# Attention values in the last mixer of a two-block network: V stationary, outputs transposed, another order of the queues

## The reference

```python
def masked_softmax(s, mask):
    s = jnp.where(mask, s.astype(jnp.float32), NEG)
    m = jnp.max(s, axis=-1, keepdims=True)
    p = jnp.where(mask, jnp.exp(s - m), 0.0)
    return p / jnp.maximum(jnp.sum(p, axis=-1, keepdims=True), 1e-30)

    proj = xn @ w_in[l]              # 1024 -> 5400: all inputs of both mixers
    y_a = hgrn2_mixer(a_q, a_f, a_i, a_g, lb_all[l], hgrn_norm_g[l])
    y_b = nsa_mixer(b_q, kc, vc, ks_, vs_, kw_, vw_, b_gate, positions, ...)
...
        # in nsa_mixer, for 8 heads of width 64 in 2 groups of 4
        o_c = p_c @ vc               # 15 compressed blocks
        o_s = p_s @ v_sel            # selected blocks
        o_w = p_w @ v_w              # window of 512
        return gb[..., 0:1] * o_c + gb[..., 1:2] * o_s + gb[..., 2:3] * o_w
...
    g_a, g_b = jnp.split(jax.nn.sigmoid(m_gate), 2, axis=-1)
    merged = g_a * (y_a @ w_br_a[l]) + g_b * (y_b @ w_br_b[l])
    h = h + merged @ w_out[l]
    hn = rmsnorm(h, norm2_g[l])
    h = h + jnp.square(jax.nn.relu(hn @ w_ff1[l])) @ w_ff2[l]
```

## Time and profile before

| | |
|---|---|
| median of 3 runs | 1398.23 us (1398.12 to 1399.13) |
| the profiled execution, its time | 1401.26 us |
| its span, first to last instruction | 1399.5 us |
| outside the span | 1.8 us |
| mean granted TensorE clock | 0.993 |
| TensorE busy | 1371.5 us, 98% |
| VectorE busy | 809.1 us, 58% |
| ScalarE busy | 680.6 us, 49% |

### The profile page before, as it was taken

One profiled execution on the slowest core, in us unless ns is written; L12 is line 12 of the kernel. 1 busy time (PEld: TensorE's weight loads), 2 busy tenths in 40 slices (PEclk: granted clock), 3 DMA queues, 4 the chain that ended last, 5 costly groups with the idle time before them and its releaser, 6 DMA issues.

```text
span 1399.5 us, 17400 instructions
## 1 busy us (share of the span) xinstructions
PE 1371.5 (98%) x6529; PEld 1125.6 (80%) x6529; DVE 809.1 (58%) x889; ACT 680.6 (49%) x877; POOL 37.5 (3%) x100
## 2 busy tenths in 40 slices
PE   8999999999999999999999999999999989999997
PEld 6888888888888888888877788888787778888886
DVE  5555566664555655444578754456676547664553
ACT  5444464454444644444467644445663555543442
POOL 2000000000000000000001100000000000000000
PEclk9999999999999999999999999999999989999999
DMA  8665656545656554555751365565553333565540
GB/s 288 212 195 185 212 179 210 178 139 184 195 191 225 180 180 150 182 187 196 240 172 55 112 208 182 187 196 200 198 181 121 107 138 121 184 237 180 180 165 30
DMA packets 160236, 247.09 MB, mean 177 GB/s; under 512 B 9086, under 2 KB 104504, under 8 KB 160184
## 3 DMA queue, kind: packets, MB, share of 16 engines
q1 hardware_dynamic: 160072, 246.33, 53.2%
q10 hardware_dynamic: 112, 0.05, 0.0%
HBM read 245.30 MB, written 1.05 MB: 176 GB/s over the span
## 4 chain that ended last, share of the span: by engine, by line
PE 95%; ACT 3%; DVE 1%; issue 0%; DMA 0%; POOL 0%; SPq 0%; POOLq 0%; ACTq 0%; DVEq 0%
PE GU L557 15%; PE GU L559 15%; PE GU L558 15%; PE DD L557 11%; PE DD L559 11%; PE DD L558 11%; PE GU L622 4%; PE TB L594 3%; PE TB L750 2%; PE GU L629 2%; ACT xh L1532 1%; PE DD L1185 0%; ACT whi L1520 0%; DMA raw<-in_w_ffn_up 0%; ACT sm L1921 0%
## 5 line engine op out<-in xcount | busy, mean ns | idle before, releaser
L2130 DVE TENSOR_TENSOR wlo<-raw,whi 128x2048 fp32r<-128x2048 f32 x224 | 509.3, 2282 | 273.4 <-ACT whi L1520 273.2
L1520 ACT ACTIVATE whi<-raw 128x2048 fp32r<-128x2048 f32 x223 | 424.2, 1908 | 176.8 <-PE DD L559 166.5
L557 PE MATMUL GU<-whi,xh 128*128 128x512 f32 (+1 forms) x944 | 373.1, 395 | 0.5 <-DVE hid L2247 0.5
L559 PE MATMUL GU<-whi,xl 128*128 128x512 f32 (+1 forms) x944 | 367.5, 389 | 0.0
L558 PE MATMUL GU<-wlo,xh 128*128 128x512 f32 (+1 forms) x944 | 366.3, 388 | 0.0
L559 PEld LDWEIGHTS GU<-whi,xl 128*128 128x128 f32 x944 | 177.5, 188 | 37.5
L557 PEld LDWEIGHTS GU<-whi,xh 128*128 128x128 f32 x944 | 177.7, 188 | 36.7 <-issue 2.1
L558 PEld LDWEIGHTS GU<-wlo,xh 128*128 128x128 f32 x944 | 177.9, 188 | 34.5
L557 PE MATMUL DD<-whi,hth 128*128 128x512 f32 x496 | 194.7, 393 | 0.0
L559 PE MATMUL DD<-whi,htl 128*128 128x512 f32 x496 | 193.2, 390 | 0.0
L558 PE MATMUL DD<-wlo,hth 128*128 128x512 f32 x496 | 193.1, 389 | 0.0
(11 more groups left out here) (300 smaller groups left out, 1082.6 us busy)
## 6 DMA issues: line engine op xcount, KB each, us to landing
raw<-in_w_ffn_down SPq DMA_DIRECT2D x88, 512.0 KB, 4.4
raw<-in_w_ffn_gate SPq DMA_DIRECT2D x86, 512.0 KB, 4.0
raw<-in_w_ffn_up SPq DMA_DIRECT2D x86, 512.0 KB, 5.0
raw<-in_w_ff SPq DMA_DIRECT2D x64, 512.0 KB, 4.4
raw<-in_w_in SPq DMA_DIRECT2D x40, 512.0 KB, 4.6
raw<-in_w_conv_in SPq DMA_DIRECT2D x24, 512.0 KB, 4.9
raw<-in_w_kv SPq DMA_DIRECT2D x16, 512.0 KB, 4.7
raw<-in_w_conv_out SPq DMA_DIRECT2D x8, 512.0 KB, 4.9
```

What stands on the lines that cost most here:

```text
L557: pe.matmul(dst, h, w_h, start=start, stop=False)
L559: return pe.matmul(dst, l, w_h, start=False, stop=stop)
L1520: nc.scalar.activation(whi[s][:, 0:size], raw[s][:, 0:size], ACT.Copy).then_inc(hi_done[s], 1)
L2130: nc.vector.tensor_tensor(wlo[s][:, 0:size], raw[s][:, 0:size], whi[s][:, 0:size].bitcast(F32), ALU.subtract).then_inc(lo_done[s], 1)
```

## The change

Five things are changed, all in the mixer stage.

1. `values(u)` makes V stationary (128 keys x 64 columns) and streams the transposed probabilities, 256 columns for the first 128 keys and 128 columns for the second. The two heads of a unit go into columns 0 to 63 and 64 to 127 of the array and so into the two halves of the PSUM partitions. There are four matmuls instead of six, and the result is the transposed output.
2. Since the rows are no longer on the partitions there, the gate over the sum is applied earlier: `normalise(u)` on VectorE multiplies the probabilities in `sm` with it, two instructions of 2 x 128 and 2 x 256 columns, and `probs_t(u, c)` waits for that (`norm_ready`) instead of for `exp_done`. `outputs(u)` becomes a copy of 128 x 256 into `yT` for units 0 to 3 and an addition for units 4 to 7; `add_outputs` is gone.
3. `block_values` is turned in the same way (four matmuls of 256 columns), the gate goes into the block probabilities, and `block_outputs(b)` is one addition of 128 x 512 for each half.
4. The attention's output is thus already transposed. The two `fill(yb, b)` with their eight transposes are gone, and `high_sums(b)` and `low_sums(b)` split it from SBUF, 128 x 512 each.
5. Group 10 of the projection accumulates in `DD` instead of `GU` (`win_bank`), which lets it go ahead of `block_values`. The orders on the three engines are written anew.

```diff
-        yb = hid[:, :, :]
+        yT = hid[:, :, :].rearrange("p t (a n) -> p (t a) n", n=S)
...
+        def win_bank(g):
+            return DD if g == 10 else GU
...
                 def probs_t(u, c):
-                    pe.wait_ge(exp_done, u + 1)
+                    pe.wait_ge(norm_ready, u + 1)
                     bank_transposes(c, [(q * P, sm[:, u % 2, c, q * P:(q + 1) * P]) for q in range(3)])
...
-                    for i in range(2):
-                        lo_ = 3 * P * i
-                        o0, o1 = (slice((2 * i + q) * 64, (2 * i + q) * 64 + 64) for q in range(2))
-                        pe.matmul(TB[:, b, o0], at[:, b, lo_:lo_ + P], vals[:, 0, :], start=True, stop=True)
-                        pe.matmul(TB[:, b, o1], at[:, b, lo_ + P:lo_ + 2 * P], vals[:, 0, :], start=True, stop=False)
-                        mm = pe.matmul(TB[:, b, o1], at[:, b, lo_ + 2 * P:lo_ + 3 * P], vals[:, 1, :], start=False, stop=True)
+                    for c in range(2):
+                        pe.matmul(TB[64 * c:64 * c + 64, b, 0:S], vals[:, 0, :], at[:, b, 3 * P * c:3 * P * c + S], start=True, stop=False)
+                    for c in range(2):
+                        mm = pe.matmul(TB[64 * c:64 * c + 64, b, P:S], vals[:, 1, :], at[:, b, 3 * P * c + S:3 * P * (c + 1)],
+                                       start=False, stop=True)
...
-                    for t in range(TT):
-                        mm = pe.matmul(GU[:, t, :], pcT[:, t * P:(t + 1) * P], vbd, start=True, stop=True)
+                    for j in range(4):
+                        mm = pe.matmul(GU[:, j // 2, S * (j % 2):S * (j % 2) + S], vbd[:, j * P:(j + 1) * P], pcT, start=True, stop=True)
...
                 compress(0, 0)
-                probs_t(3, 0)
                 compress(0, 1)
-                values(2)
                 pe.wait_ge(t_used[1], spot(base, "tk3"))
                 scores(4)
-                probs_t(3, 1)
+                values(2)
                 compress(1, 0)
                 compress(1, 1)
-                values(3)
+                probs_t(3, 0)
+                probs_t(3, 1)
                 hidden_sums(0)
                 scores(5)
                 pe.wait_ge(parts_ready, 2)
                 win(9, "a0")
                 hidden_sums(1)
-                scores(6)
+                values(3)
                 probs_t(4, 0)
                 win(9, "a1")
+                scores(6)
...
                 probs_t(6, 1)
+                win(10, "a0")
                 values(5)
                 probs_t(7, 0)
+                win(10, "a1")
                 block_probs_t()
+                probs_t(7, 1)
...
                 block_values()
-                probs_t(7, 1)
                 values(6)
                 values(7)
-                pe.wait_ge(oc_used, 1)
-                win(10, "a0")
                 pe.wait_ge(ya_ready, 1)
                 fill(ya, 0)
-                win(10, "a1")
                 fill(ya, 1)
                 win(10, "b0")
                 win(10, "b1")
-                pe.wait_ge(yb_ready, 1)
-                fill(yb, 0)
-                fill(yb, 1)
+                pe.wait_ge(yb_ready, 2)
...
                 for t in range(TT):
                     pe.wait_ge(gu_used[t], n.gu)
                 branch(0, 0)
...
+                def high_sums(b):
+                    act.wait_ge(yb_ready, b + 1)
+                    nc.scalar.activation(xh[:, 4 + 2 * b:6 + 2 * b, :], yT[:, 2 * b:2 * b + 2, :], ACT.Copy).then_inc(xh_done, 1)
...
+                def normalise(u):
                     dve.wait_ge(exp_done, u + 1)
                     chain(nc.vector.reciprocal(rdn8[:, u, :, :], den8[:, u, :, :]))
                     gv = gate_cols[:, :, 3 * 2 * j + br + 1:3 * (2 * j + 2):3].rearrange("p t i -> p i t")
                     chain(nc.vector.tensor_tensor(wgt8[:, u, :, :], rdn8[:, u, :, :], gv, ALU.mult))
+                    p4 = sm[:, b, :, :].rearrange("p c (k n) -> p c k n", n=P)
+                    for q, ks in ((0, slice(0, 1)), (1, slice(1, 3))):
+                        ins = nc.vector.tensor_tensor(p4[:, :, ks, :], p4[:, :, ks, :],
+                                                      wgt8[:, u, :, q:q + 1].unsqueeze(3).broadcast_to([P, 2, q + 1, P]), ALU.mult)
+                    ins.then_inc(norm_ready, 1)
+
+                def outputs(u):
...
+                    if br == 0:
+                        nc.vector.tensor_copy(yT[:, j, :], TB[:, b, 0:S]).then_inc(t_used[b], 1)
+                    else:
+                        dve.wait_ge(t_used[b], spot(base, f"V{j}"))
+                        nc.vector.tensor_tensor(yT[:, j, :], yT[:, j, :], TB[:, b, 0:S], ALU.add).then_inc(t_used[b], 1)
```

94 lines of the change are left out of this document (45 added, 49 removed).

## The result

The changed kernel takes 1393.35 us in the median of 8 runs (1390.72 to 1394.77), the kernel before 1398.43 us (8 runs). The ratio is 0.995, with a 95% interval from 0.9936 to 0.9963: faster, by 5.1 us in the medians. The forecast was 1392.1.

A forecast was written before the change was run, and what follows sets the result against it. TensorE, busy 98% of the span, was taken as the bound. Values -2.3, fills -0.2, waits 0, clock -2.8 and -0.8 for waits vanishing at low clock sum to -6.1 us: 1398.2 to 1392.1 us, range 1388.0 to 1396.8.

The forecast's parts named there:

- Values: Eight values units on TensorE: 10.1 us before, 1.02 us each after, 7.8 us in all, so -2.3 us.
- The rival of the loads: Values units: eight loads of V, 134 ns each, not hidden; 2.1 us a unit, +2.5 us in all, 1400.7; chance 4%.
- The rival of heads in turn: Values units: the two heads run one after the other, +3.1 for -2.3 us, 1397.5 in all; chance 8%.
- Fills: Ahead of branch(0, 0): 0.97 us of yb fills go, a 0.8 us wait for group 10's copy comes; -0.2 us.
- Waits: TensorE's waits in the mixer stage: sum 4.7 us as before, so 0 us; bounds -2 to +3.
- (a): At hidden_sums(0): TensorE waits 1.6 us for the copy of unit 3's transposes, behind a split waiting for its load.
- (b): At values(3): TensorE waits 1.6 us, its bank shared with hidden_sums(1), read behind the second split, exps(4) and a table load.
- Clock: Mixer stage: two low stretches of 3.44 us lose 3.4 us where 6.2 us were lost before; -2.8 us.
- Normalise: VectorE, between exps and transposes: some 1.0 us a unit, 8 us in all, free in amount; unit 4 closest.
- No low clock in the stage: Rival for the mixer stage: all 6.2 us of low-clock loss goes; -8.4 us in all, 1389.8; chance 14%.
- Waits take the gain: Rival: normalise or the splits end 1 to 1.5 us later at three places; +3 us, 1395.1; chance 12%.
- spreading clock: Rival: three thin places each bring a stretch like the 10.24 us one; +4.8 us in all, 1403; chance 6%.

The follow-up runs named there:

- e7: Changed kernel with both heads of a unit in the same column group, head by head; 1395.41 us, ratio 0.9976.
- e11: Kernel before without the two fills of yb, xh and xl split from hid as it lies; 1401.1 us, ratio 1.0007.
- e9: Changed kernel without normalise's two multiplications, transposes waiting for the exponentials alone; 1391.72 us, ratio 0.9936.
- e5: Changed kernel timed again without any edit, in a later group of runs; 1393.36 us, ratio 0.9957.
- e3: Changed kernel with twelve unread matmuls of 512 columns put ahead of hidden_sums(0), where TensorE waited; 1391.09 us, ratio 0.9927.
- e2: Changed kernel with the first two parts of group 10's projection moved back behind values(7); 1397.98 us, ratio 0.998.
- e1: Changed kernel's new arithmetic with the orders of the kernel before on all three engines; 1399.33 us, ratio 0.9984.
- e10: Changed kernel with normalise's multiplications done twice in each of the eight units; 1395.49 us, ratio 0.9961.

## Why the prediction was right, and where it was off

**The sign, the size and the range.** 1393.35 us for a forecast of 1392.1, within 1388.0 to 1396.8 and within the forecast's own range of times. Its condition of a unit between 0.85 and 1.15 us was not met, with 0.80. Two terms were off by more than a microsecond, and against the median they were off in opposite ways: values gave more than forecast, and the clock gave next to nothing there. That the sum came out within 1.3 us is in part luck.

**Values: -3.8 us, not -2.3.** This is the mis-sized term. Eight units are about 6.3 us (six at 0.80 or 0.81, units 6 and 7 together about 1.5) for 10.1. The mechanism held: 384 columns are 0.67 us, as one head alone in e7 shows with its 0.65 us a head, and the two heads run side by side. What failed was the price of the switch, 0.35 us a unit, taken from matmuls of 128 columns. Here it is 0.80 - 0.67 = 0.13 us. What this rest is made of, no run separates; that it was called a switch is the prediction's reading. In e7 it is 1.45 - 2 x 0.67 = 0.11 us, with one column group, so the residue doesn't come from the second group. The Trainium skill, TensorEngine Tiling (Array Packing), section Theoretical Speedup, with its 2x, would have made the term, as an estimate, -5.0 us; the measured -3.8 lies between it and the forecast. The two heads by themselves do come near it, 1.45 / 0.80 = 1.8.

**The rival of the loads** (8 x 134 ns not hidden) has fallen: a unit of 0.80 us has no room for 0.67 us of columns and 1.07 us of loads in turn. By the rule on row groups in the Trainium skill, TensorE: Matmul & The Clock Gate, Part 3, The mechanism, these loads would not overlap; this trace doesn't agree, with the same 0.80 us. The rival of heads in turn is what e7 is, and e7 is what it would have looked like.

**Fills: -0.2 us, right to the digit.** The wait ahead of branch(0, 0) is 0.80 us, released by VectorE's copy of group 10, as forecast, and e11 shows it by itself on the kernel before: 0.97 us gone, 0.83 us come.

**Waits: the sum nearly right, the parts not.** Beside the 0.8 us they are 3.05 + 0.61 + 0.34 + 0.31 = 4.3 us, forecast 4.7. (a) at hidden_sums(0) was 3.05 us for 1.6. TensorE came there at 1111.4 as in the walk (1111.5), but the load was slower. ScalarE in the changed kernel:

```profile
1106.68 0.40 ACT L1937 ACTIVATE proj<-GU 128x256 f32<-128x256 f32 x1
1112.04 1.91 ACT L1521 ACTIVATE whi<-raw 128x2048 fp32r<-128x2048 f32 x1 [4.96 <-DMA raw<-in_w_in]
1113.86 0.85 ACT L1931 ACTIVATE at<-TB 128x384 f32<-128x384 f32 x2
```

SyncE issued it at 1105.39, 6.65 us before ScalarE could start, where the row of before had 5.03. The prediction took that one row as the duration and gave a late landing to the bounds only. In the other profiles with this order at that place the wait is between 1.7 us (e9) and 3.2 (e5), so it scatters by more than the error. (b) at values(3) was 0.61 for 1.6; the waits at unit 0's values and at unit 6's transposes were 0.34 for 0.4, and none for 0.4. The 0.31 at unit 3's transposes, where the walk of the queues had no wait, is within its 0.3 for small ones.

**Clock: -3.4 us between the two profiles, forecast -2.8, but not against the median.** One stretch with 5.52 us of work instead of two with 3.44 each. The place was right, the first of the two; the second, behind wait (b), did not come; that wait was short, 0.61 us. The cause holds: e3 takes the thin stretch away and the clock stays at 1.00, e2 and e1 bring thin stretches back and the clock falls there.

The step that failed is another. The 6.2 us of low clock were read from an execution at 0.993, 3.0 us above the median, and the forecast took the saving off the median of 1398.2, as if that execution's low clock were in it. It isn't: six of the eight runs of before beside the result lie between 1398.06 and 1399.13 us, the level of the cluster at 0.996, and e11's profile at 0.996 has one low stretch of 6.8 us in the stage, as the changed kernel has. There the clock term is about 0 us for -2.8. Over many executions it is not nothing, since the kernel before is often at 0.993: the mean of its 63 runs is 1399.9 us, that of the changed kernel's 16 is 1393.1, which are 6.8 us.

The forecast also took off 0.8 us for waits that vanish at low clock; what the waits show less than before is 0.4, the difference between 4.7 and 4.3.

**Normalise** is nearly free as the change places it, 0.3 us of wait at unit 3. Its 16 records take 8.2 us for 8 forecast; VectorE's busy time grew by 5.2 us, since other steps went. That it stays hidden is the work of the orders (4.3 us of wait without them, e1). The prediction named unit 4 as the closest; e10 shows units 3 and 6, where no cover is left.

**The sum:** -3.8 - 0.2 - 0.4 - 3.4 = -7.8 us, for the 7.3 us that the marks show; the 0.5 us between them is not settled. The medians show 5.1 and 5.5 us (e5), less than the 7.9 of the two spans: the profiled execution of before was 3.0 us above its median, as the prediction said, and that of the changed kernel, 1393.31, is at its median. Without the clock the terms are -3.8 - 0.2 - 0.4 = -4.4 us, and this is what is measured at like clock: 4.5 us between the stages of e11 and the changed kernel, 5.0 us between the runs at 0.996.

**Rivals.** *No low clock in the stage* did not happen in the profiled execution, but the changed kernel's run at 0.999, 1390.72 us, comes near to it, and e3 is that case: 1391.09 us against the 1389.8 forecast for it. *Waits take the gain* happened in one place with 1.5 us and was repaid in another. Nothing bore out the *spreading clock*: no profile has more than 10.2 us of low clock in the stage, before had 13.7.
